# The second feed-forward product of a decoder layer by Strassen's scheme, with its sums on GpSimd

## The chip, the cores and the metric

The kernel runs on one core of one Trainium2 chip. The metric is the time of one execution on the device, in microseconds. The engines are TensorE (PE in the profile; its weight loads are PEld), VectorE (DVE), ScalarE (ACT), GpSimd (POOL), and SyncE (SP), which only issues loads and stores here.

## The reference, cut to what matters

One layer over 256 tokens of width 1024, float32: a mixer of attention and gated linear attention, cross-attention to 256 memory tokens, and a feed-forward block, with a layer norm behind each. The last part is what changes:

```python
D_MODEL, SEQ, D_FF = 1024, 256, 4096
DEEPNORM_ALPHA = 2.0 ** 0.25
def _sq_relu_mlp(h, w_ff1, w_ff2):
    return jnp.square(jax.nn.relu(h @ w_ff1)) @ w_ff2
ff = _sq_relu_mlp(x, w_ff1[l], w_ff2[l])
x = _layer_norm(DEEPNORM_ALPHA * x + ff, ln3_g[l], ln3_b[l])
```

## The kernel before, in words

**Precision.** Every large product is made of rounded operands (type fp32r) in three matmuls: ScalarE rounds a float32 tensor to its high part, VectorE subtracts that from the original to get the low part, and TensorE adds high x high, high x low and low x high (the helper `three`, L1374 to L1376). So each weight tile costs a load, one ScalarE pass and one VectorE pass before TensorE can use it. A "unit" is a load of 1 MB, 128 partitions x 2048; four buffers `raw` hold them, and a load waits until the low part of the unit four before it is made.

**The first product** (`ff1`, hidden = x @ w_ff1) goes by groups of 512 hidden columns. For each of four 128-wide blocks, 8 matmuls with 512 moving columns multiply the high weights by x's high and low parts at once, into the two halves of a bank (L1774), and 8 with 256 columns add the low weights (L1781). Banks 0 to 3 take the four blocks. ScalarE copies the small half out (L829), VectorE adds it to the other half from the bank (L1292), squares the positive part (L1295), and the two make high and low parts of the hidden blocks (L833, L1301).

**The second product** (`ff2`) adds each group's part to four banks, 4 to 7: two halves of the tokens (t) by two halves of the output columns (n), with four hidden tiles (k) and three matmuls each: 48 matmuls of 512 columns a group, 8 groups. The banks are started (seeded) with ALPHA x.

**Order.** Each engine runs its own list of instructions, with semaphores between them. The groups alternate: first product of group g+1, second product of group g; the weights of one are prepared while TensorE works on the other. The first group's first product is made in another form (`tokens`, hid0 and hid1) with a transpose. Six groups lie in a loop on each engine. GpSimd has no part in this stage but the inverse roots of the norms (L532). After the last matmul the layer norm of each half of the tokens ends the kernel (L1148 to L1165), and four stores.

## Time and profile before

| | |
|---|---|
| median of 3 runs | 406.27 us (405.71 to 406.28) |
| profiled execution, its span (its whole time is not on the page) | 404.4 us |
| TensorE busy | 397.4 us, 98% |
| VectorE busy | 286.5 us, 71% |
| ScalarE busy | 208.2 us, 51% |
| GpSimd busy | 64.7 us, 16% |
| loads and stores | 75.68 MB, mean 187 GB/s |

Busy time is the time in which an engine executes something; the span runs from the first instruction to the last. The chain that ended last is followed back from the last instruction, at each step to what released it. A matmul's duration (0.39 us) overlaps the next one's, so what counts for TensorE is the distance between starts.

### The profile page before, as it was taken

What the parts mean: (1) busy time and instruction counts of PE and PEld (TensorE: products, weight loads), DVE (VectorE), ACT (ScalarE), POOL (GpSimd) and SP (SyncE); (2) the same over time, 40 slices, a digit from 0 to 9 for tenths busy, and PEclk for the clock granted to TensorE, in tenths of its full rate; (3) what the DMA queues carried; (4) which work ended last, traced back from release to release, by engine and by line L of the source; (5) the groups of instructions that cost most, each with busy time, mean ns of one, the idle gap of its engine ahead of it and who ended that gap; (6) DMA issues with size and microseconds to landing.
All of it is one profiled execution on the core that took longest, in us unless ns stands there. A gap on an engine that the chain in (4) does not pass through costs nothing.

```text
span 404.4 us, 5680 instructions
## 1 busy us (share of the span) xinstructions
PE 397.4 (98%) x2148; PEld 341.3 (84%) x2148; DVE 286.5 (71%) x376; ACT 208.2 (51%) x295; POOL 64.7 (16%) x61
## 2 busy tenths in 40 slices
PE   9999999999999999999999999999999999999993
PEld 6888888888988888899888888888888888888882
DVE  5599584999987896878658858474656466574826
ACT  6666569566464627565743366353534434354500
POOL 2059300047951004000006000000000000000000
PEclk9999999999999999999999999999999999999999
DMA  8998727635635380827166173746465654644002
GB/s 287 376 352 281 254 106 264 255 105 174 243 109 205 108 309 0 311 105 245 68 209 201 46 273 117 256 155 212 199 207 207 207 207 150 237 141 198 0 0 104
DMA packets 31195, 75.68 MB, mean 187 GB/s; under 512 B 1510, under 2 KB 2886, under 8 KB 31174
## 3 DMA queue, kind: packets, MB, share of 16 engines
q1 hardware_dynamic: 30784, 75.24, 53.5%
q8 instruction: 13, 0.21, 0.2%
q10 hardware_dynamic: 390, 0.17, 0.2%
q14 instruction: 8, 0.07, 0.1%
HBM read 74.35 MB, written 1.05 MB: 186 GB/s over the span
## 4 chain that ended last, share of the span: by engine, by line
PE 98%; DVE 1%; DVEq 0%; issue 0%
PE bank L1374 18%; PE bank L1376 18%; PE bank L1375 18%; PE bank L1774 13%; PE bank L1448 12%; PE bank L1781 7%; PE bank L1452 6%; PE bank L1600 2%; PE bank L1380 1%; PE bank L1440 1%; PE bank L1554 1%; PE bank L1587 0%; PE bank L1653 0%; PE bank L1705 0%; PE bank L1546 0%; PE bank L1545 0%
## 5 line engine op out<-in xcount | busy, mean ns | idle before, releaser
L907 DVE TENSOR_TENSOR w_lo<-raw,w_hi 128x2048 fp32r<-128x2048 f32 x36 | 84.5, 2352 | 12.9 <-ACT w_hi L556 12.8
L556 ACT CAST w_hi<-raw 128x2048 fp32r<-128x2048 f32 x38 | 72.1, 1913 | 15.4 <-PE bank L1376 14.3
L1309 DVE TENSOR_TENSOR w_lo<-raw,w_hi 128x2048 fp32r<-128x2048 f32 x24 | 54.4, 2289 | 30.4 <-ACT w_hi L844 30.4
L1374 PE MATMUL bank<-w_hi,actB 128*128 128x512 f32 x192 | 75.6, 394 | 0.0
L1375 PE MATMUL bank<-w_lo,actB 128*128 128x512 f32 x192 | 74.9, 390 | 0.0
L1376 PE MATMUL bank<-w_hi,actB 128*128 128x512 f32 x192 | 74.8, 390 | 0.0
L844 ACT CAST w_hi<-raw 128x2048 fp32r<-128x2048 f32 x24 | 45.4, 1917 | 34.4 <-PE bank L1376 34.4
L1774 PE MATMUL bank<-actA,w_hi 128*128 128x512 f32 x224 | 52.2, 390 | 0.0
L1774 PEld LDWEIGHTS bank<-actA,w_hi 128*128 128x128 f32 x224 | 42.0, 188 | 8.7
L1376 PEld LDWEIGHTS bank<-w_hi,actB 128*128 128x128 f32 x192 | 36.1, 188 | 7.6
L1374 PEld LDWEIGHTS bank<-w_hi,actB 128*128 128x128 f32 x192 | 36.1, 188 | 7.2
L1375 PEld LDWEIGHTS bank<-w_lo,actB 128*128 128x128 f32 x192 | 36.1, 188 | 6.8
L1374 PE MATMUL bank<-w_hi,actA 128*128 128x512 f32 x96 | 38.0, 396 | 0.0
L1376 PE MATMUL bank<-w_hi,actA 128*128 128x512 f32 x96 | 37.5, 391 | 0.0
L1375 PE MATMUL bank<-w_lo,actA 128*128 128x512 f32 x96 | 37.5, 390 | 0.0
L532 POOL TENSOR_TENSOR rstd<-vareps,minus_half 128x1 f32<-128x1 f32 x6 | 3.3, 546 | 194.9 <-DVE vareps L1155 194.8
L1448 PE MATMUL bank<-actA,w_hi 128*128 128x512 f32 x140 | 34.3, 391 | 0.0
L1448 PEld LDWEIGHTS bank<-actA,w_hi 128*128 128x128 f32 x140 | 25.4, 188 | 4.6
L1781 PEld LDWEIGHTS bank<-actA,w_lo 128*128 128x128 f32 x224 | 27.8, 192 | 0.5
L1781 PE MATMUL bank<-actA,w_lo 128*128 128x256 f32 x224 | 28.0, 283 | 0.0
L829 ACT COPY att<-bank 128x256 f32<-128x256 f32 x28 | 9.6, 372 | 30.4 <-PE bank L1781 30.4
L1292 DVE TENSOR_TENSOR att<-bank,att 128x256 f32<-128x256 f32 x28 | 11.1, 421 | 16.3 <-ACT att L829 16.2
(198 smaller groups left out, 591.3 us busy)
## 6 DMA issues: line engine op xcount, KB each, us to landing
raw<-in_w_ff SPq DMA_DIRECT2D x32, 1024.0 KB, 5.4
raw<-in_w_in SPq DMA_DIRECT2D x10, 1024.0 KB, 6.4
raw<-in_w_xkv SPq DMA_DIRECT2D x8, 1024.0 KB, 5.0
raw<-in_w_mix_o SPq DMA_DIRECT2D x4, 1024.0 KB, 4.8
raw<-in_w_xq SPq DMA_DIRECT2D x4, 1024.0 KB, 4.9
raw<-in_w_xo SPq DMA_DIRECT2D x4, 1024.0 KB, 5.0
raw<-in_lead SPq DMA_DIRECT2D x6, 384.0 KB, 5.1
probs<-in_ln_g SPq DMA_DIRECT2D x3, 512.0 KB, 6.3
```

The lines of the kernel that those rows point to most:

```text
L556: act.copy(dst, half_view(u)).then_inc(hi_done, 1)
L844: act.copy(w_hi[:, (C_LOOP + k) % 2, half, :], raw[:, u % RAW, :]).then_inc(hi_done, 1)
L907: dve.tensor_tensor(dst, half_view(u), hi_part.bitcast(f32), ALU.subtract).then_inc(lo_done, 1)
L1292: dve.tensor_tensor(v, bank[2 * f + m][:, 0:S], v, ALU.add).then_inc(bank_free[2 * f + m], 1)
L1309: dve.tensor_tensor(w_lo[:, c % 2, half, :], raw[:, u % RAW, :], w_hi[:, c % 2, half, :].bitcast(f32), ALU.subtract).then_inc(lo_done, 1)
L1374: pe.matmul(dst, stat[0], mov[0], start=start, stop=False, skip_group_check=on)
L1375: pe.matmul(dst, stat[0], mov[1], start=False, stop=False, skip_group_check=on)
L1376: return pe.matmul(dst, stat[1], mov[0], start=False, stop=stop, skip_group_check=on)
L1448: pe.matmul(dst[:, :].rearrange("p (h s) -> p h s", h=2), weight(c, k, m * P, (m + 1) * P)[0], act[:, :, k, :], start=k == 0, stop=False, ...
L1452: return pe.matmul(dst[:, S:2 * S], weight(c, k, m * P, (m + 1) * P)[1], act[:, 0, k, :], start=False, stop=k == 7, skip_group_check=True)
L1774: pe.matmul(bank[m][:, :].rearrange("p (h s) -> p h s", h=2), w_hi[:, par, k // 4, a:a + P], actA[:, :, k, :], start=k == 0, stop=False, s ...
L1781: i = pe.matmul(bank[m][:, S:2 * S], w_lo[:, par, k // 4, a:a + P], actA_hi[:, k, :], start=False, stop=k == 7, skip_group_check=True)
```

## The change

Hidden tiles are taken in 16 pairs of k. For a pair, the left operand is a 2 x 2 arrangement of 128 x 128 blocks (two halves of the tokens, A1 and A2, by two k) and the right one is 2 x 2 blocks of 128 x 512. Instead of eight block products, seven are made (Strassen's scheme in Winograd's form), from raw blocks and from sums: S1 to S4 of hidden blocks, T1 to T4 of weight blocks. Each of the seven products adds up over the pairs in a bank of its own (0 to 6), and at the end VectorE combines the seven into the four corners of the output. The last pair is multiplied directly into the corners, with 24 matmuls. So pairs 0 to 14 have 21 matmuls for 24.

- GpSimd makes the sums T1 to T4 of each pair (four of 128 x 512) and S1 to S4 (four of 128 x 128), and adds the two halves of each first product's block (128 x 256, twice).
- ScalarE and VectorE make high and low parts of the sums too. The weights of the raw blocks B11, B22, B21 are rounded as one piece of 1536 columns; B12 itself is never multiplied but in the last pair. Rounding of the first product's weights goes in halves of 1024.
- The first product is made block by block, two blocks a pair (`up_block`), set between the products of the second. All blocks but one use bank 7, since seven banks hold products; ScalarE copies the whole bank into SBUF (`empty`) and so frees it.
- The weights are laid out on the host so that each load's partition row is contiguous. The loads are as many and as large as before.
- The loops are written out. The last norm takes the second half of the tokens first.

```diff
-G = 8
+PAIRS = 16
+A21, A11, A22, A12 = range(4)
+RAW_A, SUM_A = {"A11": 0, "A22": 1, "A12": 2}, {"S1": 3, "S2": 4, "S3": 5, "S4": 6}
+A_AT = {**RAW_A, **SUM_A}
+B_AT = {"B11": 0, "B22": 1, "B21": 2, "T1": 3, "T2": 4, "T4": 5, "T3": 6}
+PRODUCTS = {"P1": ("A11", "B11"), "P2": ("A12", "B21"), "P3": ("S4", "B22"), "P4": ("A22", "T4"),
+            "P5": ("S1", "T1"), "P6": ("S2", "T2"), "P7": ("S3", "T3")}
+P_BANK = {"P1": 0, "P2": 3, "P3": 2, "P4": 1, "P5": 4, "P6": 5, "P7": 6}
+FIRST_ORDER = ["P1", "P2", "P4", "P5", "P7", "P6", "P3"]
+ORDER = ["P1", "P2", "P3", "P4", "P5", "P6", "P7"]
+LAST_ORDER = ["P1", "P2", "P3", "P6", "P5", "P7", "P4"]
...
+FF_UNITS = [("down", 0), ("up", 2), ("up", 3), ("down", 1)]
+for _q in range(1, PAIRS - 2):
+    FF_UNITS += [("up", _q + 3), ("down", _q + 1)]
...
+        blocks = [flatB[:, 0:1792], flatB[:, 1792:3584], shared("probsT", 0, 1792)]
+        sums_w = probs[:, 0:2048]
+        down_hi = [again[:, at["values"]:at["values"] + 3584], w_hi[:, 0].rearrange("p h n -> p (h n)")[:, 0:3584]]
+        down_lo = [again[:, at["values"] + 3584:at["values"] + 7168],
+                   w_lo[:, 0].rearrange("p h n -> p (h n)")[:, 0:3584]]
...
+            def weight_sum(q, name):
+                u = ff_unit("down", q)
+                b12, b11, b22, b21 = [half_view(u)[:, n * 512:(n + 1) * 512] for n in range(4)]
+                t1, t2, t4, t3 = [sums_w[:, n * 512:(n + 1) * 512] for n in range(4)]
+                if name == "T1":
+                    pool.wait_ge(raw_in[u % RAW], raw_count(u))
+                    if q == 0:
+                        wait_full(pool, "cpv3")
+                    else:
+                        pool.wait_ge(wsum_lo, 2 * (q - 1) + 1)
+                    pool.tensor_tensor(t1, b12, b11, ALU.subtract).then_inc(wsum_made, 1)
+                elif name == "T2":
+                    pool.wait_ge(wsum_made, 4 * q + 1)
+                    pool.tensor_tensor(t2, b22, t1, ALU.subtract).then_inc(wsum_made, 1)
+                elif name == "T4":
+                    pool.wait_ge(wsum_made, 4 * q + 2)
+                    if q > 0:
+                        pool.wait_ge(wsum_lo, 2 * (q - 1) + 2)
+                    pool.tensor_tensor(t4, t2, b21, ALU.subtract).then_inc(wsum_made, 1)
+                else:
+                    pool.tensor_tensor(t3, b22, b12, ALU.subtract).then_inc(wsum_made, 1)
+            def add_halves(p, m):
+                n = 2 * (p - 2) + m
+                pool.wait_ge(up_free, n + 1)
+                pool.tensor_tensor(emptied[:, m, 0:S], emptied[:, m, 0:S], emptied[:, m, S:2 * S], ALU.add)\
+                    .then_inc(halves_added, 1)
+            def hidden_sums(p):
+                a21, a11, a22, a12, s1, s2, s3, s4 = [hidden[p % 2][:, n * P:(n + 1) * P] for n in range(8)]
+                if p < 2:
+                    wait_out(pool, "ht1")
+                else:
+                    pool.wait_ge(hidden_done, p - 1)
+                    pool.wait_ge(asum_lo, p - 1)
+                pool.tensor_tensor(s1, a21, a22, ALU.add).then_inc(asum_made, 1)
+                pool.wait_ge(asum_made, 4 * p + 1)
+                pool.tensor_tensor(s2, s1, a11, ALU.subtract).then_inc(asum_made, 1)
+                pool.tensor_tensor(s3, a11, a21, ALU.subtract).then_inc(asum_made, 1)
+                pool.wait_ge(asum_made, 4 * p + 2)
+                pool.tensor_tensor(s4, a12, s2, ALU.subtract).then_inc(asum_made, 1)
...
+            for q in range(1, PAIRS - 2):
+                hidden_sums(q + 1)
+                weight_sum(q + 1, "T1")
+                add_halves(q + 2, 0)
+                weight_sum(q + 1, "T2")
+                weight_sum(q + 1, "T4")
+                weight_sum(q + 1, "T3")
+                add_halves(q + 2, 1)
...
+            def empty(p, m):
+                n = 2 * (p - 2) + m
+                act.wait_ge(up_full, n + 1)
+                if n >= 2:
+                    act.wait_ge(hidden_done, p - 2)
+                act.copy(emptied[:, m], bank[6 if n == 1 else 7][:, :]).then_inc(up_free, 1)
...
+            for q in range(1, PAIRS - 2):
+                hidden_high(q + 1)
+                up_high(q + 3, 0)
+                empty(q + 2, 0)
+                asum_high(q + 1)
+                down_high(q + 1)
+                up_high(q + 3, 1)
+                empty(q + 2, 1)
+                wsum_high(q + 1, 0)
+                wsum_high(q + 1, 1)
...
-            def square(f, small, free):
-                for m in range(2):
-                    v = relu[:, f, m * S:(m + 1) * S]
-                    dve.wait_ge(small_done, small + (2 * f + m + 1))
-                    dve.tensor_tensor(v, bank[2 * f + m][:, 0:S], v, ALU.add).then_inc(bank_free[2 * f + m], 1)
-                for m in range(2):
-                    dve.wait_ge(bank_free[2 * f + m], free[2 * f + m])
-                dve.scalar_tensor_tensor(relu[:, f, :], relu[:, f, :], 0.0, relu[:, f, :], ALU.max, ALU.mult)\
-                    .then_inc(sq_done, 1)
...
+            def wsum_low(q, half):
+                cut = slice(1536 + 1024 * half, 2560 + 1024 * half)
+                dve.wait_ge(wsum_hi, 2 * q + half + 1)
+                dve.tensor_tensor(down_lo[q % 2][:, cut], sums_w[:, 1024 * half:1024 * (half + 1)],
+                                  down_hi[q % 2][:, cut].bitcast(f32), ALU.subtract).then_inc(wsum_lo, 1)
+            def square(p):
+                dve.wait_ge(halves_added, 2 * (p - 2) + 2)
+                dve.wait_ge(a_lo, p - 1)
+                dve.wait_ge(asum_lo, p - 1)
+                v = emptied[:, :, 0:S]
+                dve.scalar_tensor_tensor(hidden[p % 2][:, 0:512].rearrange("p (m s) -> p m s", m=2), v, 0.0, v,
+                                         ALU.max, ALU.mult).then_inc(hidden_done, 1)
...
+            for q in range(1, PAIRS - 2):
+                wsum_low(q, 0)
+                wsum_low(q, 1)
+                hidden_low(q + 1)
+                up_low(q + 3, 0)
+                asum_low(q + 1)
+                down_low(q + 1)
+                up_low(q + 3, 1)
+                square(q + 2)
+            wsum_low(PAIRS - 2, 0)
...
+            b = product("P2")
+            dve.wait_ge(p1_copied, 1)
+            dve.tensor_tensor(b, b, first_product, ALU.add).then_inc(corner_done, 1)
+            link(dve.tensor_tensor(first_and_sixth, product("P6"), first_product, ALU.add))
+            link(dve.tensor_tensor(with_fifth, product("P5"), first_and_sixth, ALU.add))
+            b = product("P3")
+            dve.tensor_tensor(b, b, with_fifth, ALU.add).then_inc(corner_done, 1)
+            link(dve.tensor_tensor(with_seventh, product("P7"), first_and_sixth, ALU.add))
+            link(dve.scalar_tensor_tensor(left_rest, X[:, 0, 0:512], ALPHA, with_seventh, ALU.mult, ALU.add))
+            dve.tensor_tensor(bank[P_BANK["P7"]][:, :], product("P5"), left_rest, ALU.add).then_inc(corner_done, 1)
+            b = product("P4")
+            dve.tensor_tensor(b, with_seventh, b, ALU.subtract).then_inc(corner_done, 1)
...
+            def up_block(p, m, between=None):
+                n = 2 * (p - 2) + m
+                b = bank[6 if n == 1 else 7]
+                if n == 0:
+                    wait_out(pe, "yt11")
+                elif n == 1:
+                    wait_out(pe, "yt10")
+                else:
+                    pe.wait_ge(up_free, 1 if n == 2 else n)
+                hi, lo = (v[:, 1, p % 2, :].rearrange("p (k n) -> p k n", k=8) for v in (w_hi, w_lo))
+                for k in range(8):
+                    if m == 0 and k % 4 == 0:
+                        pe.wait_ge(up_hi, 2 * (p - 2) + k // 4 + 1)
+                    pe.matmul(b[:, :].rearrange("p (h s) -> p h s", h=2), hi[:, k, m * P:(m + 1) * P], actA[:, :, k, :],
+                              start=k == 0, stop=False, skip_group_check=True)
+                if between is not None:
+                    between()
+                for k in range(8):
+                    if m == 0 and k % 4 == 0:
+                        pe.wait_ge(up_lo, 2 * (p - 2) + k // 4 + 1)
+                    i = pe.matmul(b[:, S:2 * S], lo[:, k, m * P:(m + 1) * P], actA_hi[:, k, :],
+                                  start=False, stop=k == 7, skip_group_check=True)
+                i.then_inc(up_full, 1)
+            def multiply(q, names, last=False):
+                for name in names:
+                    a, b = PRODUCTS[name]
+                    pe.wait_ge(a_lo, q + 1)
+                    if a in SUM_A:
+                        pe.wait_ge(asum_lo, q + 1)
+                    if B_AT[b] < 3:
+                        pe.wait_ge(down_raw_lo, q + 1)
+                    else:
+                        pe.wait_ge(wsum_lo, 2 * q + (B_AT[b] - 3) // 2 + 1)
+                    to = bank[P_BANK[name]]
...
+                    fresh = q == 0 and name in ("P1", "P5", "P6", "P7")
+                    cut_a, cut_b = slice(A_AT[a] * P, (A_AT[a] + 1) * P), slice(B_AT[b] * 512, (B_AT[b] + 1) * 512)
+                    i = three(to[:, :], [blocks[q % 3][:, cut_a], blocks[q % 3][:, 896:1792][:, cut_a]],
+                              [v[q % 2][:, cut_b] for v in (down_hi, down_lo)], fresh, False, on=True)
+                    if last:
+                        i.then_inc(product_done, 1)
+                if not last and name == "P7" or name == "P3" and q == 0:
+                    i.then_inc(pair_used, 1)
+            up_block(2, 0, between=lambda: transpose_hidden(0))
+            transpose_hidden(1)
+            up_block(2, 1)
+            multiply(0, FIRST_ORDER)
+            for q in range(1, PAIRS - 2):
+                up_block(q + 2, 0)
+                multiply(q, ORDER[:3])
+                up_block(q + 2, 1)
+                multiply(q, ORDER[3:])
+            multiply(PAIRS - 2, LAST_ORDER, last=True)
+            pe.wait_ge(a_lo, PAIRS)
+            pe.wait_ge(up_lo, 2 * (PAIRS - 2) + 2)
+            final = blocks[(PAIRS - 1) % 3]
+            for n, (name, t, c) in enumerate([("P2", 1, 1), ("P3", 1, 0), ("P7", 0, 0), ("P4", 0, 1)]):
+                pe.wait_ge(corner_done, n + 1)
+                for m in range(2):
+                    block_at = (2 * m + t) * P
+                    i = three(bank[P_BANK[name]][:, :], [final[:, at0 + block_at:at0 + block_at + P] for at0 in (0, 896)],
+                              [v[:, 1, 0, m * 1024 + c * 512:m * 1024 + (c + 1) * 512] for v in (w_hi, w_lo)],
+                              False, m == 1, on=True)
+                i.then_inc(corner_full, 1)
```

How the order of instructions moves. TensorE, inside the stage: before, one group's first product runs over four banks without a break, and its second product follows.

```order
L1774 MATMUL bank<-actA,w_hi 128x512 [waits bank_free1]
L1774 MATMUL bank<-actA,w_hi 128x512 x7
L1774 MATMUL bank<-actA,w_hi 128x512 [waits bank_free2]
L1774 MATMUL bank<-actA,w_hi 128x512 x7
L1774 MATMUL bank<-actA,w_hi 128x512 [waits bank_free3]
L1774 MATMUL bank<-actA,w_hi 128x512 x7
L1781 MATMUL bank<-actA,w_lo 128x256 x32
```

TensorE, now, from the second up block of one pair on (`up_free` is raised by ScalarE's copy out of bank 7; `wsum_lo`, `asum_lo` and `a_lo` by VectorE's low parts of T, of S and of the raw hidden blocks):

```order
L1963 MATMUL bank<-actA,w_hi 128x512 [waits up_free]
L1963 MATMUL bank<-actA,w_hi 128x512 x7
L1970 MATMUL bank<-actA,w_lo 128x256 x8
L1558 MATMUL bank<-w_hi,actB 128x512 [waits wsum_lo,a_lo]
L1559 MATMUL bank<-w_lo,actB 128x512
L1560 MATMUL bank<-w_hi,actB 128x512
L1558 MATMUL bank<-w_hi,actB 128x512 [waits wsum_lo,asum_lo,a_lo]
L1559 MATMUL bank<-w_lo,actB 128x512
L1560 MATMUL bank<-w_hi,actB 128x512
```

Each block of the first product now waits for the copy of the block before it, and each product names the low parts that it needs.

VectorE, one half of a group before, inside its loop:

```order
L1292 TENSOR_TENSOR att<-bank,att 128x256 [waits small_done]
L1294 REGISTER_ALU
L1295 SCALAR_TENSOR_TENSOR att<-att 128x512 [waits bank_free3,bank_free2]
L1308 REGISTER_ALU
L1309 TENSOR_TENSOR w_lo<-raw,w_hi 128x2048 [waits hi_done]
L1299 REGISTER_ALU
L1301 TENSOR_TENSOR actB<-att,actB 128x512 [waits hid_hi]
```

VectorE, one pair now (`const` here is the tensor that the bank was copied into, `probs` the T sums, `qk` the hidden blocks and S sums):

```order
L1437 TENSOR_TENSOR w_lo<-probs,w_hi 128x1024 [waits wsum_hi] x2
L1452 TENSOR_TENSOR actB<-qk,actB 128x384 [waits a_hi]
L1424 TENSOR_TENSOR w_lo<-raw,w_hi 128x1024 [waits up_hi]
L1457 TENSOR_TENSOR actB<-qk,actB 128x512 [waits asum_hi]
L1430 TENSOR_TENSOR again<-raw,again 128x1536 [waits down_raw_hi]
L1424 TENSOR_TENSOR w_lo<-raw,w_hi 128x1024 [waits up_hi]
L1445 SCALAR_TENSOR_TENSOR qk<-const 128x512 [waits asum_lo,a_lo,halves_added]
```

The additions that read a bank are gone from VectorE's list, and every instruction left in it reads tensors in SBUF only.

GpSimd, which before had only three inverse roots after the last of its rounding work, now has ten instructions for each pair:

```order
L604 TENSOR_TENSOR qk<-qk 128x128 [waits asum_lo,hidden_done]
L606 TENSOR_TENSOR qk<-qk 128x128 [waits asum_made]
L607 TENSOR_TENSOR qk<-qk 128x128
L609 TENSOR_TENSOR qk<-qk 128x128 [waits asum_made]
L578 TENSOR_TENSOR probs<-raw 128x512 [waits wsum_lo,raw_in1]
L593 TENSOR_TENSOR const<-const 128x256 [waits up_free]
L581 TENSOR_TENSOR probs<-raw,probs 128x512 [waits wsum_made]
L586 TENSOR_TENSOR probs<-probs,raw 128x512 [waits wsum_lo,wsum_made]
L588 TENSOR_TENSOR probs<-raw 128x512
L593 TENSOR_TENSOR const<-const 128x256 [waits up_free]
```

They stand between the square of one pair, which the first of them waits for, and the square of the next, which waits for the last.

## Rows read from the trace of the kernel before

**Rows 1.** The page: busy time by engine, and the chain that ended last.

```profile
PE 397.4 (98%) x2148; PEld 341.3 (84%) x2148; DVE 286.5 (71%) x376; ACT 208.2 (51%) x295; POOL 64.7 (16%) x61
...
PE 98%; DVE 1%; DVEq 0%; issue 0%
```

**Rows 2.** Chain in order of time: start us, duration us, engine, tile, line, count.

```profile
232.43 5.45 PE bank L1774 x24
...
299.31 7.25 PE bank L1774 x32
...
321.30 7.25 PE bank L1774 x32
...
372.54 3.83 PE bank L1781 x32
```

**Rows 3.** Groups by line from 230 to 400: busy us, mean ns, idle before.

```profile
L1309 DVE TENSOR_TENSOR w_lo<-raw,w_hi 128x2048 fp32r<-128x2048 f32 x24 | 54.4, 2289 | 30.4 <-ACT w_hi L844 30.4
...
L844 ACT CAST w_hi<-raw 128x2048 fp32r<-128x2048 f32 x24 | 45.4, 1917 | 34.4 <-PE bank L1376 34.4
...
L1301 DVE TENSOR_TENSOR actB<-att,actB 128x512 fp32r<-128x512 f32 x14 | 9.7, 689 | 4.8 <-ACT actB L833 4.8
...
L833 ACT CAST actB<-att 128x512 fp32r<-128x512 f32 x14 | 8.7, 624 | 8.9 <-DVE att L1295 8.9
...
L671 ACT ACTIVATE bank<-X 128x512 f32<-128x512 f32 x4 | 2.2, 602 | 0.0
```

**Rows 4.** Groups by line, whole span, GpSimd's longer forms.

```profile
L516 POOL TENSOR_TENSOR w_lo<-raw,w_hi 128x1024 fp32r<-128x1024 f32 x4 | 9.8, 2472 | 56.1 <-ACT w_hi L556 54.0 <-DVE X L1165 2.1
...
L497 POOL TENSOR_TENSOR qk<-gla,qk 128x256 f32<-128x256 f32 x1 | 0.8, 753 | 0.0
```

**Rows 5.** Timeline around 100, 105 and 115: start us, duration us, instruction.

```profile
100.13 2.28 DVE L907 TENSOR_TENSOR w_lo<-raw,w_hi 128x2048 fp32r<-128x2048 f32 x1
...
100.75 2.24 POOL L495 TENSOR_TENSOR qk<-gla,qk 128x256 f32<-128x256 f32 x1 [0.59 <-PE bank L1600]
...
104.69 2.29 DVE L907 TENSOR_TENSOR w_lo<-raw,w_hi 128x2048 fp32r<-128x2048 f32 x1
104.90 2.78 POOL L495 TENSOR_TENSOR qk<-gla,qk 128x256 f32<-128x256 f32 x1
...
115.15 2.55 POOL L511 TENSOR_TENSOR gla<-gla,gnorm 128x512 f32<-128x512 f32 x2
...
116.55 3.29 DVE L907 TENSOR_TENSOR w_lo<-raw,w_hi 128x2048 fp32r<-128x2048 f32 x1 [1.49 <-ACT w_hi L556]
```

**Rows 6.** The same view around 25 and from 210.

```profile
24.68 5.26 POOL L469 TENSOR_SCALAR probsT<-const 128x384 f32<-128x384 f32 x3 [21.92 <-DMA const<-in_consts]
25.03 2.31 DVE L907 TENSOR_TENSOR w_lo<-raw,w_hi 128x2048 fp32r<-128x2048 f32 x1
...
210.80 2.29 DVE L907 TENSOR_TENSOR w_lo<-raw,w_hi 128x2048 fp32r<-128x2048 f32 x1 [4.96 <-ACT w_hi L556]
...
212.66 2.69 POOL L516 TENSOR_TENSOR w_lo<-raw,w_hi 128x1024 fp32r<-128x1024 f32 x1 [53.99 <-ACT w_hi L556]
...
215.96 2.41 POOL L516 TENSOR_TENSOR w_lo<-raw,w_hi 128x1024 fp32r<-128x1024 f32 x1
...
216.61 1.40 DVE L1165 SCALAR_TENSOR_TENSOR X<-bank,rstd,probsT 128x512 f32<-128x512 f32 x2
```

**Rows 7.** The end: timeline, then a stretch (us, busy by engine, granted clock).

```profile
397.77 0.39 PE L1376 MATMUL bank<-w_hi,actB 128*128 128x512 f32 x1
398.20 0.70 DVE L1148 BATCH_NORM_STATS2 stats<-bank 128x6 f32<-128x512 f32 x1 [1.07 <-PE bank L1376]
...
400.56 1.40 DVE L1165 SCALAR_TENSOR_TENSOR X<-bank,rstd,probsT 128x512 f32<-128x512 f32 x2
...
402.50:403.00 0.50, 0.00 (x0) 0.00 (x0) 0.00 (x0) 0.00 (x0) 0.00 (x0) 0.63 1.03 377
```

**Rows 8.** The page's loads: KB each, us to landing.

```profile
raw<-in_w_ff SPq DMA_DIRECT2D x32, 1024.0 KB, 5.4
```

More of the change, by code:

```diff
@@ L144 @@
              10: "mo11", 11: "xv11", 12: "xq11", 13: "xq3", 15: "xo11", C_FF1_0: "hid1"}
-ROWS_END = {9: 1, 14: 2, C_FF2_0: 3}
-FF_BASE = [sum(b == bank for b, _ in FILL.values()) for bank in range(8)]
+ROWS_END = {9: 1, 14: 2}
 def build(nc, x, lead, memT, w_in, w_glr, w_gate_up, b_gate, gla_norm_g, w_mix_o, ln1_g, ln1_b, w_xq, w_xkv,
@@ new lines, in _ @@
+            inverse_root(0, 0, 0)
+            inverse_root(0, 1, 1)
+            pool.wait_ge(ln_done, 4)
+            for half in range(2):
+                lo_half(unit(12, 1), half)
+            lo_half(unit(C_FF1_0, 1), 0)
+            inverse_root(1, 0, 0)
+            lo_half(unit(C_FF1_0, 1), 1)
+            wait_out(pool, "yt01")
+            pool.wait_ge(xT_hi, 6)
+            sl = (slice(None), slice(4, 8), slice(0, P))
+            pool.tensor_tensor(actA_lo[sl], yT_half, actA_hi[sl].bitcast(f32), ALU.subtract)\
+                .then_inc(yT_lo, 1)
@@ new lines, in hidden_high, with asum_high @@
+            def hidden_high(p):
+                if p < 2:
+                    wait_out(act, "ht1")
+                else:
+                    act.wait_ge(hidden_done, p - 1)
+                if p >= 3:
+                    act.wait_ge(pair_used, p - 2)
+                width = 384 if p < PAIRS - 1 else 512
+                act.copy(blocks[p % 3][:, 0:width], hidden[p % 2][:, 512 - width:512]).then_inc(a_hi, 1)
+            def asum_high(p):
+                act.wait_ge(asum_made, 4 * p + 4)
+                act.copy(blocks[p % 3][:, 384:896], hidden[p % 2][:, 512:1024]).then_inc(asum_hi, 1)
@@ L876, in _ @@
[L876 to L892 removed]
+            act.wait_ge(ln_done, 8)
@@ L895, in _ @@
+            act.copy(first_product, bank[P_BANK["P1"]][:, :]).then_inc(p1_copied, 1)
         @block.vector
@@ L1355, in _ @@
-            for t in range(2):
-                layer_norm(2, t, [(bank[4 + 2 * t + c], (bank_full[4 + 2 * t + c], FF_BASE[4 + 2 * t + c] + 1), bank_free[4 + 2 * t + c])
-                                  for c in range(2)])
+            up_low(3, 0)
+            hidden_low(0)
+            hidden_low(1)
+            asum_low(0)
+            down_low(1)
+            asum_low(1)
+            up_low(3, 1)
+            square(2)
+            for q in range(1, PAIRS - 2):
[7 more added lines that the diff above has]
+                square(q + 2)
@@ L1805, in need @@
-            def need(c):
-                return [lo_count(unit(c, half)) for half in range(2)]
-            ff1(C_FF1_1 % 2, need(C_FF1_1), FF_BASE, between=transpose_hidden)
-            ff2(0, C_FF2_0 % 2, need(C_FF2_0), first=True)
-            with pe.Fori(0, G // 2 - 1) as i:
-                for g in range(2):
-                    c = C_LOOP + 2 * g
-                    ff1(c % 2, [i * 8 + n for n in need(c)], [i * 2 + (n + 1 + g) for n in FF_BASE])
-                    ff2(1 - g, (c + 1) % 2, [i * 8 + n for n in need(c + 1)], i * 4 + (2 + 2 * g))
```

389 lines of the change are left out of this document (192 added, 197 removed).

## The prediction, on record before the kernel was run

> **What bounds the kernel now.** I read the page's busy shares first, then its chain of waits, then the chain in order of time, and only then the helpers. TensorE is busy for 397.4 of 404.4 us and the chain that ended last lies on it for 98% [rows 1]. In the feed-forward stage the chain repeats every 22.0 us (321.30 − 299.31) with nothing but matmuls in it [rows 2]; a 512-column matmul follows the next after 7.25/32 = 0.2266 us, a 256-column one after 3.83/32 = 0.120 us. A stage group holds two pairs of hidden tiles, so a pair costs 11.0 us of TensorE. VectorE and ScalarE wait there for TensorE, not the other way: 30.4 us of idle time before the low parts, 34.4 us before the high parts [rows 3]. GpSimd is busy for 64.7 us of the whole span. So matmuls taken out shorten the end as long as the helpers keep up, and the whole question is whether they do.
>
> **What the change takes off TensorE.** Each pair had 8 block products of 3 matmuls; 15 of the 16 pairs now have 7. That is 45 matmuls fewer: 45 × 0.2266 = 10.2 us. A pair is then 16 × 0.2266 + 16 × 0.120 + 21 × 0.2266 = 10.3 us. This is the whole gain on offer, 404.4 − 10.2 = 394.2.
>
> **What each pair costs the helpers.** Durations of forms that the trace lacks I take between its rows. VectorE: 2048 wide is 2.29, 512 wide 0.69 [rows 3], so 1.22 for 1024, 1.76 for 1536, 0.56 for 384. A pair has four of 1024 (two weight halves, two halves of the T sums), one of 1536, one of 384, the S sums and the square at 512: 4.88 + 1.76 + 0.56 + 1.38 = 8.6 us. ScalarE: 2048 is 1.92, 512 is 0.62, the copy of a bank 0.60 [rows 3]; four of 1.05, 1.49, 0.52, 0.62 and two bank copies: 8.0 us. GpSimd: four T sums of 512, two additions of the halves at 256, four S sums of 128. 512 wide is 2.55/2 = 1.27 [rows 5], 256 wide is 0.75, 1024 wide 2.4 to 2.7 [rows 4]; 128 wide isn't in the trace: it is at least half of the 0.59 that 256 columns hold the memory (below), and at most the 0.75 of a whole 256 wide one. I take 0.31 held and 0.45 in all, on the line through 256 and 512: 5.1 + 1.5 + 1.8 = 8.4 us. Each is under 10.3 us, so three separate engines would just keep up.
>
> **They are not separate.** All of GpSimd's new instructions read two tensors in SBUF, and so do all eight of VectorE's per pair; the two banks' additions that VectorE read from PSUM are gone to ScalarE and GpSimd. The trace shows what such pairs do to each other [rows 5]. VectorE's low part runs from 100.13 to 102.41; GpSimd's product starts at 100.75, takes 2.24 instead of 0.75 and ends at 102.99, 0.58 after VectorE. Again at 104.90: 2.78, ending 0.70 after VectorE's end at 106.98. The other way round, GpSimd is busy until 117.70, and the low part that VectorE issued at 116.55 takes 3.29 instead of 2.29 and ends 2.14 later. At 212.66 GpSimd's 1024 wide piece ends at 215.35, 2.26 after VectorE's [rows 6]. So they take turns by whole instructions; only about 0.1 of start-up overlaps. Where VectorE reads one bank of PSUM there is no loss: 1.40 for two at 216.61 beside GpSimd's 2.41 at 215.96 [rows 6]. Against it stands one place: VectorE's 2.31 at 25.03 wasn't held up by GpSimd's one-input scaling from 24.68 [rows 6]; but that form is not in the new loop.
>
> The Trainium skill (SBUF — State Buffer, "Who interferes with whom") says that a VectorE instruction with two SBUF inputs and a GpSimd instruction that reads SBUF share an interface, and that the first one keeps it for the whole instruction. By that rule taken literally a pair is 8.6 + 8.4 = 17.0 us; by the rows, where start-up overlaps, it is less, and the sum goes by the rows.
>
> Held times from those rows: VectorE 2.14 per 2048 columns, so 7040 columns a pair are 7.35 us. GpSimd 2.26 per 1024, 0.59 per 256, so 1.15, 0.59 and 0.31: 4.6 + 1.18 + 1.24 = 7.0 us. Together 14.4 us a pair, if no moment is lost, against 10.3 of TensorE.
>
> **The period worked out.** Zero is the end of a square. VectorE's next low part (first half of T) goes at once, to 1.1; then they alternate: S1 to 1.4, second half of T 2.5, S2 2.8, low of the raw blocks 3.2, S3 3.5, a weight half 4.6, S4 4.9. ScalarE rounds the S sums 5.0 to 5.6. GpSimd's T1 to 6.2, low of the S sums 6.7, first addition of halves 7.3, the 1536 wide low part 8.9, T2 10.1, the other weight half 11.1, T4 12.3, T3 13.55, second addition 14.3, square 14.4 to 15.05. So I take 15.05 us a pair; the ends are 14.4 and 17.0. TensorE waits 4.75 of it, in two places: about 1 before the first up block and 3.7 before the second, since every up block but one writes bank 7 and ScalarE's copy out of it stands behind the rounding that follows the square.
>
> **The sum.** Before the loop little changes: TensorE starts the next up group at 232.3 [rows 2], does two blocks (5.5), the transposes (0.8) and pair 0 (21 × 0.2266 = 4.8) to 243.4, with 0.5 of waiting for the S sums. The helpers are behind by then. The last transposed block is out of its bank at about 236.6; GpSimd, taking turns, has eight S sums (5.2, to 241.8), two additions of halves (1.3), T4 and T3 beside a VectorE piece (3.2, to 246.3), and the square of pair 2 ends at 247.0. Twelve more periods of 15.05 give 427.6. From there the last square 15.05, two T low parts and the last raw one (3.0, GpSimd now idle), eight combinations of 0.65 (5.25) of which the corners' matmuls hide none at the end of VectorE's queue, two norms of 4.5 and 4.4 (stats 1.3, two small ones 0.35, 1.4, 1.4, as in the old tail [rows 7]), and from VectorE's end to the end of the span 404.4 − 401.96 = 2.4 [rows 7]: 34.6, span 462.2. In place of the old tail of 6.4 us behind the last matmul it is about 9, because VectorE combines products when TensorE could already be done. Other way: 394.2 + 13 × 4.75 = 456, + 2.7 tail, + 3 waited in the last pair = 462. The page gives the profiled execution no time but its span of 404.4, 1.9 under the median 406.27; with that added the forecast is 464. Loads: 1 MB lands in 5.4 us [rows 8] and a pair needs two, each asked for a full period ahead: nothing. A weight row is now contiguous, which can only help what is hidden.
>
> **Rivals.** (1) Taking turns does not hold for these instructions: then helpers at 8.0 to 8.6 of 10.3 keep up, TensorE sets the end, 394.2 + 2.7 of tail + 1 + 1.9 = 400, faster. For: the place at 25.03; against: four places of just these forms. (2) They take turns only in part, or the small sums cost less than pro rata: 12.7 a pair, 464 − 13 × 2.35 = 433. (3) No start-up overlaps, or 128-wide sums cost their upper bound: 17.0 a pair, 464 + 25 = 489. (4) The clock. TensorE's last matmul ends at 398.16; the mean granted clock from 402.50 to 403.00 is 0.63 [rows 7], so it fell from its full 2.4 GHz to the lower level of 1.2 at about 402.6, 4.5 us later. A wait of 3.7 us per pair is near to that. If it fell in each, an up block of 2.8 us would be 5.5; TensorE has 4.75 us of slack in a pair, so one block costs little, but at half clock throughout a pair is 20.6 us: somewhere between 464 and 530, I put 495. The Trainium skill (TensorE: Matmul & The Clock Gate, "The HAM clock gate") has idle time as the cause of just this fall; the row agrees, and no row of before shows a wait inside the loop long enough to try it.
>
> **How the numbers follow.** Forecast 464 with 0.76, for which 455 (no moment lost) to 480 is the likely range; (1) 0.04, (2) 0.06, (3) 0.07, (4) 0.07. Range 446 to 488: it leaves out (1), (2) and about half of (3) and (4), near 2 in 10. A difference of 0.2% (0.8 us) is about what a measurement tells from none. Faster only by (1): 0.04; within 0.2%: 0.01, for something between (1) and (2); slower 0.95.
>
> **What would show it.** Right: in the loop GpSimd's 512 wide sums last well over 1.27 on average, VectorE's 1024 wide ones over 1.22, and their ends never fall inside one another; both are busy or waiting nearly all of the period; a period near 15 us; TensorE's share falls to some 84% of the span (387 of 462 us), with its waits on the bank that ScalarE empties. Wrong: a period of 10.3 with the durations of the rows (rival 1); a granted clock under 1 in the loop (rival 4); or TensorE waiting mostly for a load.

## The result, and the profile after

The changed kernel takes 466.5 us (466.2 to 466.8, 4 runs), the kernel before 406.13 us beside it: a ratio of 1.149, 95% interval 1.148 to 1.151. The forecast was 464. The profiled execution has a span of 464.4 us, against 462.2 worked out.

The page of the changed kernel, busy time by engine and then the shares of the chain that ended last, answers to [rows 1]:

```profile
PE 411.7 (89%) x2103; PEld 344.6 (74%) x2103; DVE 355.1 (76%) x416; ACT 247.8 (53%) x357; POOL 269.1 (58%) x209
...
PE 50%; POOL 35%; DVE 6%; issue 6%; DMA 1%; ACT 1%; DVEq 0%; POOLq 0%
```

The 45 matmuls are gone (2148 to 2103), and so is the chain that lay on TensorE for 98%: 35% of the time to the end is now GpSimd's. Its groups and VectorE's in the loop, by line, from 245 to 445 us (busy us, mean ns, idle before):

```profile
L1424 DVE TENSOR_TENSOR w_lo<-raw,w_hi 128x1024 fp32r<-128x1024 f32 x27 | 51.7, 1915 | 0.0
L581 POOL TENSOR_TENSOR probs<-raw,probs 128x512 f32<-128x512 f32 x13 | 36.6, 2819 | 0.0
L586 POOL TENSOR_TENSOR probs<-probs,raw 128x512 f32<-128x512 f32 x14 | 29.8, 2128 | 1.0
...
L593 POOL TENSOR_TENSOR const<-const 128x256 f32<-128x256 f32 x26 | 25.0, 961 | 0.0
...
L609 POOL TENSOR_TENSOR qk<-qk 128x128 f32<-128x128 f32 x13 | 18.7, 1437 | 0.0
...
L1437 DVE TENSOR_TENSOR w_lo<-probs,w_hi 128x1024 fp32r<-128x1024 f32 x14 | 18.3, 1348 | 0.0
L578 POOL TENSOR_TENSOR probs<-raw 128x512 f32<-128x512 f32 x13 | 17.0, 1309 | 0.0
```

Equal forms have unequal durations: GpSimd's sums of 512 columns take 1.31 (T1), 2.13 (T4) or 2.82 us (T2), a sum of 128 columns (S4) takes longer than the T1 of 512, and VectorE's subtraction of 1024 columns takes 1.35 or 1.92. The work sets the shortest of each; what is above it is waiting inside the instruction, as the experiments below show. The timeline of one period shows whom each waits for (start us, duration us, instruction, idle before it):

```profile
338.74 0.69 DVE L1445 SCALAR_TENSOR_TENSOR qk<-const 128x512 f32<-128x512 f32 x1 [3.15 <-POOL const L593]
339.35 2.61 DVE L1437 TENSOR_TENSOR w_lo<-probs,w_hi 128x1024 fp32r<-128x1024 f32 x2
...
339.51 1.37 POOL L604 TENSOR_TENSOR qk<-qk 128x128 f32<-128x128 f32 x1 [0.80 <-DVE qk L1445]
...
341.46 2.11 PE L1963 MATMUL bank<-actA,w_hi 128*128 128x512 f32 x8 [2.84 <-ACT const L949]
...
346.49 1.97 DVE L1430 TENSOR_TENSOR again<-raw,again 128x1536 fp32r<-128x1536 f32 x1 [0.24 <-ACT again L931]
346.81 2.82 POOL L581 TENSOR_TENSOR probs<-raw,probs 128x512 f32<-128x512 f32 x1
...
347.93 2.14 PE L1963 MATMUL bank<-actA,w_hi 128*128 128x512 f32 x8 [0.67 <-ACT const L949]
348.38 2.32 DVE L1424 TENSOR_TENSOR w_lo<-raw,w_hi 128x1024 fp32r<-128x1024 f32 x1
...
349.70 2.15 POOL L586 TENSOR_TENSOR probs<-probs,raw 128x512 f32<-128x512 f32 x1
```

T2 (L581) is issued at 346.81, inside VectorE's 1536-wide instruction, which ends at 348.46; T2 ends at 349.63, 1.17 after it. The weight half that VectorE issued at 348.38 then takes 2.32 and ends at 350.70, 1.07 after T2; T4 ends at 351.85, 1.15 after that. In the trace the recorded spans overlap, but the ends stand one behind the other, each by about the time that its own work takes: what overlaps is the waiting. It is the pattern of [rows 5], now all through the loop. The square of the next pair starts at 353.84, so the period is 15.10 us.

What the engines wait for, from 245 to 445 us (total us, times, longest):

```profile
DVE qk L1445 <- POOL const L593: 40.8, 13, 3.2
PE bank L1963 <- ACT const L949: 36.7, 16, 3.0
```

And busy time by engine over three periods (stretch, its us, busy, granted clock in the third number from the right):

```profile
338.74:353.84 15.10, 11.21 (x53) 8.74 (x53) 10.71 (x8) 7.46 (x10) 14.14 (x10) 1.00 0.35 136
353.84:368.93 15.09, 12.26 (x53) 9.95 (x53) 10.69 (x8) 7.47 (x10) 14.13 (x10) 0.89 0.37 143
368.93:384.04 15.11, 11.22 (x53) 8.75 (x53) 10.73 (x8) 7.46 (x10) 14.15 (x10) 1.00 0.37 136
```

GpSimd is busy 14.1 of 15.1 us. The 13 periods of the loop last 15.08 to 15.12 us, the last one 15.00, whatever the clock of TensorE.

### The profile page after: what moved, and what is told of

Its sections match the earlier page's. It is cut to its first block, busy times and chain, and to the rows that moved or that the text cites. A ratio compares the mean times of both kernels' runs of the same rounds, so it can differ in the third digit from the quotient of the medians.

```text
span 464.4 us, 5838 instructions
## 1 busy us (share of the span) xinstructions
PE 411.7 (89%) x2103; PEld 344.6 (74%) x2103; DVE 355.1 (76%) x416; ACT 247.8 (53%) x357; POOL 269.1 (58%) x209
## 4 chain that ended last, share of the span: by engine, by line
PE 50%; POOL 35%; DVE 6%; issue 6%; DMA 1%; ACT 1%; DVEq 0%; POOLq 0%
PE bank L1632 10%; PE bank L1558 9%; PE bank L1560 9%; PE bank L1559 9%; POOL probs L581 8%; POOL probs L586 6%; PE bank L1636 5%; POOL qk L609 4%; POOL qk L604 4%; POOL qk L606 4%; POOL probs L578 4%; POOL probs L588 4%; DVE qk L1445 2%; POOL const L593 2%; PE bank L1784 1%
## 5 line engine op out<-in xcount | busy, mean ns | idle before, releaser
L1963 PE MATMUL bank<-actA,w_hi 128*128 128x512 f32 x224 | 69.2, 459 | 36.7 <-ACT const L949 36.7
L1963 PEld LDWEIGHTS bank<-actA,w_hi 128*128 128x128 f32 x224 | 47.7, 220 | 53.8 <-ACT const L949 43.6
L1040 DVE TENSOR_TENSOR w_lo<-raw,w_hi 128x2048 fp32r<-128x2048 f32 x30 | 70.6, 2359 | 5.8 <-ACT w_hi L643 5.6
L643 ACT CAST w_hi<-raw 128x2048 fp32r<-128x2048 f32 x32 | 60.7, 1913 | 11.5 <-PE bank L1560 9.3
L1424 DVE TENSOR_TENSOR w_lo<-raw,w_hi 128x1024 fp32r<-128x1024 f32 x30 | 57.4, 1916 | 0.0
L1558 PE MATMUL bank<-w_hi,actB 128*128 128x512 f32 x107 | 42.5, 397 | 0.0
L1559 PE MATMUL bank<-w_lo,actB 128*128 128x512 f32 x107 | 41.8, 391 | 0.0
L1560 PE MATMUL bank<-w_hi,actB 128*128 128x512 f32 x107 | 41.7, 390 | 0.0
L581 POOL TENSOR_TENSOR probs<-raw,probs 128x512 f32<-128x512 f32 x15 | 39.6, 2639 | 0.2
L1632 PE MATMUL bank<-actA,w_hi 128*128 128x512 f32 x140 | 34.4, 391 | 0.0
L586 POOL TENSOR_TENSOR probs<-probs,raw 128x512 f32<-128x512 f32 x15 | 31.1, 2074 | 1.1
L919 ACT CAST w_hi<-raw 128x1024 fp32r<-128x1024 f32 x30 | 31.2, 1044 | 0.0
```

The source lines that it names most:

```text
L581: pool.tensor_tensor(t2, b22, t1, ALU.subtract).then_inc(wsum_made, 1)
L586: pool.tensor_tensor(t4, t2, b21, ALU.subtract).then_inc(wsum_made, 1)
L643: act.copy(dst, half_view(u)).then_inc(hi_done, 1)
L1040: dve.tensor_tensor(dst, half_view(u), hi_part.bitcast(f32), ALU.subtract).then_inc(lo_done, 1)
L1424: dve.tensor_tensor(w_lo[:, 1, p % 2, cut], half_view(ff_unit("up", p))[:, cut], w_hi[:, 1, p % 2, cut].bitcast(f32), ALU.subtract).then_i ...
L1558: pe.matmul(dst, stat[0], mov[0], start=start, stop=False, skip_group_check=on)
```

## The experiments

The theory: VectorE's and GpSimd's instructions that read two tensors in SBUF (the memory on the chip that the engines work from; the banks lie in another one, PSUM) take turns by whole instructions, and the period is made up of the times for which each holds the other off, with little else. The rivals: GpSimd's own chain is too long whatever VectorE does; VectorE has too much work; TensorE's order with one bank for the up blocks costs the time; or the reading is not what matters, only that GpSimd is at work. The kernel before took 405.7 to 405.8 us beside these runs. Periods are from one square to the next.

**One side made short.** In the first, GpSimd's ten instructions of a pair stay, but cover 16 columns; the rest is left out.

```diff
+                if q > 0:
+                    b12, b11, b22, b21, t1, t2, t4, t3 = [v[:, 0:16] for v in (b12, b11, b22, b21, t1, t2, t4, t3)]
...
-                pool.tensor_tensor(emptied[:, m, 0:S], emptied[:, m, 0:S], emptied[:, m, S:2 * S], ALU.add)\
+                pool.tensor_tensor(emptied[:, m, 0:16], emptied[:, m, 0:16], emptied[:, m, S:S + 16], ALU.add)\
```

> From the second use of each buffer on, GpSimd's sums and additions are cut to 16 columns (the rest of them isn't computed); the order, the waits and VectorE's work stay. Theory A (GpSimd's and VectorE's two-input instructions exclude each other): VectorE's 1024 wide low parts fall from a mean of 1.9 to 1.22 us, the 1536 wide from 1.97 to 1.76, the period of a pair from 15.1 to TensorE's 10.3, the time to 466.5 - 13 x 4.8 = 404 or a little less (400 to 405), the wait for bank 7 nearly gone. Rival B (the single bank 7 and the chain of hand-overs between engines set the period, whatever the durations): above 12.5 us a pair, 433 or more.

In the second, VectorE's subtractions and the square are cut so, and GpSimd's work is whole.

```diff
-                cut = slice(half * 1024, (half + 1) * 1024)
+                cut = slice(half * 1024, half * 1024 + 16)
...
-                width = 384 if p < PAIRS - 1 else 512
+                width = 16
```

> VectorE's low parts and its square are cut to 16 columns in the stage of pairs (the rest isn't computed), GpSimd keeps its whole work. Theory A: GpSimd's 512 wide sums take 1.30 each (now 1.31, 2.82, 2.13, 1.39), the 128 wide 0.45 (now 0.77 to 1.44), the 256 wide 0.75 (now 0.97); 8.4 us in all, plus hand-overs: 10.3 a pair, 400 to 405 us. Rival C (GpSimd is that slow by itself in this stage, from its operands or from the loads that write the same buffers): its durations stay, period about 14, time about 452.

And in the third both.

> Both cuts at once (neither GpSimd's sums nor VectorE's low parts are computed beyond 16 columns): what TensorE alone makes of the new order. Period 10.3. The prediction's parts: 394.2 + 2.7 for the longer tail + 1 + 1.9 outside of the span = 400. If TensorE's saving of 45 matmuls did not come, or the order cost more by itself (the wait for bank 7), over 406.

Measured: 399.35 us (ratio 0.984, 0.982 to 0.986), 399.38 (0.984, 0.982 to 0.986) and 399.2 (0.984, 0.982 to 0.986). The first two lie 0.6 us under their range of 400 to 405. Cutting either side alone gives all of it back, and cutting both gives nothing more. Neither engine is the bound with its own work: it is the two together. At a period of 10.4 us TensorE is the bound again, and these 399 us are what the fewer matmuls are worth, near the 400 of rival 1. Groups by line of the first (GpSimd short), from 245 to 370 us:

```profile
L1428 DVE TENSOR_TENSOR w_lo<-raw,w_hi 128x1024 fp32r<-128x1024 f32 x25 | 30.8, 1231 | 0.0
...
L613 POOL TENSOR_TENSOR qk<-qk 128x16 f32<-128x16 f32 x12 | 14.3, 1194 | 0.0
```

of the second (VectorE short):

```profile
L1424 DVE TENSOR_TENSOR w_lo<-raw,w_hi 128x16 fp32r<-128x16 f32 x25 | 20.1, 805 | 18.3 <-ACT w_hi L919 18.3
...
L593 POOL TENSOR_TENSOR const<-const 128x256 f32<-128x256 f32 x24 | 17.8, 740 | 17.8 <-ACT const L949 17.8
L578 POOL TENSOR_TENSOR probs<-raw 128x512 f32<-128x512 f32 x13 | 17.0, 1309 | 0.0
...
L609 POOL TENSOR_TENSOR qk<-qk 128x128 f32<-128x128 f32 x13 | 6.0, 462 | 0.0
```

and of the third:

```profile
L611 POOL TENSOR_TENSOR qk<-qk 128x16 f32<-128x16 f32 x12 | 2.7, 223 | 0.0
...
L1428 DVE TENSOR_TENSOR w_lo<-raw,w_hi 128x16 fp32r<-128x16 f32 x25 | 4.4, 176 | 19.3 <-ACT w_hi L923 19.3
```

Undisturbed, VectorE's 1024 columns are 1.23 us and GpSimd's 128, 256 and 512 columns are 0.46, 0.74 and 1.30 (worked out before: 1.22; 0.45, 0.75, 1.27). The clearest rows are those of 16 columns: a sum of GpSimd takes 0.22 us when VectorE's instructions are short too and S4 takes 1.19 beside VectorE's full ones; VectorE's subtraction takes 0.18 and, beside GpSimd's full sums, 0.81. So each waits for the other. These durations also rule out that the period is only a chain of semaphores from engine to engine: such waits stand in the profile as idle time ahead of an instruction, and here the instructions themselves are longer.

**Reading, or only being at work?** From the second pair on, GpSimd's sums are replaced by fills of a scratch tile, which read nothing, in the same chain of semaphores; the sums are left out.

```diff
+                    i = pool.memset(scratch[:, :], 0.0)
...
-                    pool.tensor_tensor(t2, b22, t1, ALU.subtract).then_inc(wsum_made, 1)
+                    pool.tensor_tensor(t2, b22, t1, ALU.subtract).then_inc(wsum_made, 1) if q == 0 else fill(4, wsum_made, 4 * q + 2)
```

> GpSimd's sums are replaced by fills of a scratch tensor that take about as long (4 fills of 352 columns for a 512 wide sum, 2 for an addition of halves, 1 for a 128 wide sum; the sums are not computed), with the same waits: GpSimd is as busy and reads nothing. Theory A with the page's condition that GpSimd must read: VectorE's 1024 wide low parts 1.22, period 10.3 to 11.2 (GpSimd's own list), time 402 to 414. If any busy GpSimd hinders VectorE, whether it reads or not: low parts stay near 1.9, about 15 a pair, 460 and more.

Measured: 423.7 us (1.044, 1.042 to 1.046), period 12.0. That is above the 402 to 414 expected, so the expectation missed. A second version has 14 fills a pair in place of 24.

> As e4_gpsimd_writes_only, in which GpSimd fills a scratch tile in place of its sums in SBUF from the second pair on (so the sums are left out), but with 14 fills of a pair in place of 24. There 24 linked fills took the whole period of 12.00 us, 0.50 us each. If GpSimd's own chain was what held that kernel at 423.7 us, 14 fills take 7.0 us of a pair and the period falls to TensorE's 10.4 us, as in the two kernels with short sums: 399 to 401 us. If a GpSimd that only writes does hinder VectorE, the period stays between 10.8 and 12, 405 to 420 us, and VectorE's 1024-wide instruction shows more than 1.22 us in its mean.

Measured: 399.95 us (0.985, 0.984 to 0.987), period 10.4. Groups by line of the kernel with 24 fills, from 245 to 370 us:

```profile
L575 POOL MEMSET scratch<- 128x352 f32 x252 | 98.9, 393 | 26.8 <-DVE qk L1460 7.8
...
L1439 DVE TENSOR_TENSOR w_lo<-raw,w_hi 128x1024 fp32r<-128x1024 f32 x21 | 25.6, 1217 | 0.0
```

and of the one with 14, from 310 to 400:

```profile
L575 POOL MEMSET scratch<- 128x352 f32 x92 | 36.1, 393 | 33.3 <-ACT const L964 22.2 <-DVE qk L1460 4.7
...
L1439 DVE TENSOR_TENSOR w_lo<-raw,w_hi 128x1024 fp32r<-128x1024 f32 x13 | 15.8, 1219 | 0.0
```

The miss was my filler, not the theory: 24 linked fills of 0.50 us each were a chain of 12 us. In both, VectorE's 1024 columns take 1.22 us, and no fill takes less than 0.387 or more than 0.403 us: a GpSimd that only writes does not hold VectorE up, and is not held up.

**One input in place of two.** GpSimd scales one tensor, 430, 240 and 128 columns wide, in place of its sums.

```diff
-                    pool.tensor_tensor(t4, t2, b21, ALU.subtract)
+                    pool.tensor_scalar(t4[:, 0:430], t2[:, 0:430], 1.0, None, ALU.mult)
```

> GpSimd's sums are replaced by scalings with one input, shorter so that each should last as long alone (430 columns for a 512 wide sum, 240 and 128 for the others; the sums are not computed). If a GpSimd instruction that reads one tensor holds VectorE off for its whole length, the period stays about 15 and VectorE's 1024 wide low parts near 1.9. If it holds only for a short part, as the one place at 25 us in the trace of before looks, VectorE's durations are near 1.3, GpSimd still waits for VectorE, and the period is 11 to 13, the time 410 to 440.

Measured: 435.4 us (1.073, 1.071 to 1.075), period 12.85. Groups by line, 245 to 370 us:

```profile
L1424 DVE TENSOR_TENSOR w_lo<-raw,w_hi 128x1024 fp32r<-128x1024 f32 x20 | 28.6, 1431 | 0.0
L586 POOL TENSOR_SCALAR probs<-probs 128x430 f32<-128x430 f32 x10 | 18.7, 1870 | 0.7
...
L604 POOL TENSOR_SCALAR qk<-qk 128x128 f32<-128x128 f32 x10 | 14.3, 1434 | 7.3 <-DVE qk L1445 7.3
```

It lies between: 1.43 us in place of 1.92 for VectorE's weight half, 1.87 in place of 2.13 for what stands in T4's place. GpSimd itself still waits: the 128 columns of L604 take 1.43, with two inputs 1.37. So a GpSimd instruction with one input holds VectorE off too, for a part of the time. That fits neither the place in [rows 6] where VectorE's 2.31 us lost nothing nor the full turn-taking. What sets the part is not shown.

**Fewer turns.** TensorE adds the two halves of an up block in the same half of the bank, so GpSimd has eight instructions a pair in place of ten and ScalarE copies half a bank; the sums are unchanged.

```diff
-                    pe.matmul(b[:, :].rearrange("p (h s) -> p h s", h=2), hi[:, k, m * P:(m + 1) * P], actA[:, :, k, :],
+                    for act in (actA_hi, actA_lo):
+                        pe.matmul(b[:, 0:S], hi[:, k, m * P:(m + 1) * P], act[:, k, :],
```

> The changed kernel with one part of GpSimd's work gone by another way: the first product's small terms are added by TensorE into the same half of the bank (three matmuls of 256 columns for one of 512 and one of 256), so the two additions of halves go and ScalarE copies 256 columns. The result is whole. TensorE 10.5 a pair. Theory A: two turns fewer, 2 x 0.59 held and about 0.1 each of hand-over: 15.1 - 1.4 = 13.7 a pair, 448 us. Rival B (bank 7): ScalarE's copy comes back by 0.2 earlier only, 14.9 a pair, 463.

Measured: 444.7 us (1.096, 1.094 to 1.098), period 13.56. The two turns are worth 1.54 us a pair. 2 × 0.59 held is 1.18 of it; the other 0.36 isn't traced to its place. Rival B's 14.9 a pair is ruled out.

**The sums on VectorE.** GpSimd has nothing in the loop.

```diff
-                    pool.tensor_tensor(t2, b22, t1, ALU.subtract).then_inc(wsum_made, 1)
+                    dve.tensor_tensor(t2, b22, t1, ALU.subtract).then_inc(wsum_made, 1)
```

> All sums and additions of halves move from GpSimd to VectorE, which then has 18 instructions a pair and GpSimd none. The result is whole. Theory A: since the two were never beside each other, and VectorE needs 1.04 ns a column where GpSimd holds the memory for 2.2, one engine alone is faster: 4 x 1.13 + 1.66 + 0.46 + 1.2 + 2.4 + 0.8 + 0.68 and 0.5 of own waits = 12.2 to 12.4 a pair, 466.5 - 13 x 2.7 = 431 us (426 to 438), faster than with both engines and slower than before. If the two engines had worked side by side, taking the work of one to the other could not shorten the period: 15.1 or more.

Measured: 426.6 us (1.052, 1.050 to 1.053), period 12.14. One engine that does all the work is 40 us faster than two that share it. With that and the edit before it:

> As v1_sums_on_vector, and the additions of halves left to TensorE as in e6_no_halves. The result is whole. VectorE's list: 11.7 a pair, 466.5 - 13 x 3.4 = 422 us; TensorE's 10.5 isn't reached, so still slower than before.

Measured: 415.7 us (1.025, 1.023 to 1.026), period 11.35. And with ScalarE taking the relu out of the bank and squaring:

```diff
-                act.copy(emptied[:, m, 0:S], bank[6 if n == 1 else 7][:, 0:S]).then_inc(up_free, 1)
+                act.activation(emptied[:, m, 0:S], bank[6 if n == 1 else 7][:, 0:S], ACT.Relu).then_inc(up_free, 1)
...
+                    act.activation(hidden[p % 2][:, 0:512].rearrange("p (m s) -> p m s", m=2), emptied[:, :, 0:S],
+                                   ACT.Square).then_inc(hidden_done, 1)
```

> The whole result is computed: as in v3_no_halves (all sums on VectorE, TensorE adds the small terms in the same half of the bank), and now ScalarE also takes the relu while it empties the bank and squares the hidden block; VectorE has no square. In v3_no_halves VectorE was busy 11.28 of a period of 11.35 us, and the square took 0.60 us of it (square at 246.35, next instruction at 246.95). If VectorE is the bound there, the period falls to 11.35 - 0.60 = 10.75 us and the time to 415.7 - 12 x 0.6 = 408.5 us (406 to 411), which is near the kernel before (405.8) but not clearly under it. If instead TensorE's feed or ScalarE's queue sets the period (ScalarE gets one instruction of about 0.6 us more on 7.05 us busy), it stays above 11.2 and the time above 413 us.

Measured: 409.1 us (1.008, 1.006 to 1.009), period 10.75. Two periods of it, in the columns of the stretches above:

```profile
330.55:341.29 10.74, 10.74 (x70) 9.74 (x69) 10.67 (x16) 7.60 (x10) 0.00 (x0) 1.00 0.52 197
341.29:352.05 10.76, 10.76 (x70) 9.74 (x69) 10.69 (x16) 7.61 (x11) 0.00 (x0) 1.00 0.50 194
```

VectorE is busy 10.67 of 10.74 us, and TensorE has no idle time left either. This loop is shorter than the 11.0 us a pair of [rows 2], yet the kernel is 3 us slower than before. The end takes part of it: the span ends 8.5 us after the last matmul (399.21 to 407.7), since VectorE combines the seven products there, and 6.2 us in the kernel before (398.16 to 404.4, [rows 7]). Where the loop begins, TensorE is idle 2.2 us between 232 and 252, and in the last pair it waits 1.5 and 0.4 us more for VectorE; it did neither before. That is 6.4 us lost against about 13 × 0.25 = 3.2 won in the loop. No version with a whole result is faster than the kernel before. What is left to take from VectorE in the last one's loop is some 0.2 us a pair: by the distances of [rows 2], TensorE needs 48 × 0.120 + 21 × 0.2266 = 10.5 with the halves added by its matmuls.

## Why the prediction was right, step by step

**TensorE's saving.** Right. With the helpers out of the way the kernels take 399.2 to 399.4 us and the period is 10.4, against 400 and 10.3.

**Three engines that would just keep up.** Right, now as measured durations: 4 × 1.30 + 2 × 0.74 + 4 × 0.46 = 8.5 us of GpSimd a pair (8.4 worked out), and a period of TensorE's length (10.4) when VectorE's work is short, and the same the other way.

**Turn-taking.** Right, and it is the cause: shown by cutting either side, by the sum of 16 columns that takes 1.19 us, by the fills that read nothing, and by the 40 us won when one engine does the work of both. GpSimd's ten instructions last 14.1 us a pair in place of 8.5. The Trainium skill (SBUF — State Buffer, "Who interferes with whom") has the first one keep the interface for its whole instruction. The order of ends agrees; the literal sum of 17.0 us does not, since 15.10 was measured. What it leaves out is the start-up beside the other's hold; the prediction's held times, without it, gave 14.4.

**The period.** 15.10 against 15.05. The order of turns was worked out right in the places that carry the time: T2 and T4 behind VectorE's 1536- and 1024-wide pieces, the second addition ahead of the square. The waits of TensorE came out at 0.67 and 2.84 us before the two up blocks, where the prediction had about 1 and 3.7. Its idle time in a full-clock period is 15.10 − 11.21 = 3.9 in place of 4.75. Part of the difference is that the busy time counts each matmul to its own end, 0.39 us, where the next follows after 0.23: ahead of a wait that adds 0.16 to it.

**The start.** The one term that was clearly mis-sized: the square of pair 2 ends at 248.80 in place of 247.0. The sum had it behind GpSimd's T3, and there it stands, but T3 ends at 248.26 in place of 246.3. GpSimd's and VectorE's lines of the timeline:

```profile
241.36 2.95 POOL L593 TENSOR_TENSOR const<-const 128x256 f32<-128x256 f32 x2
241.70 2.01 DVE L1430 TENSOR_TENSOR w_lo<-raw,w_hi 128x1536 fp32r<-128x1536 f32 x1 [1.05 <-ACT w_hi L931]
243.63 1.22 DVE L1457 TENSOR_TENSOR actB<-qk,actB 128x512 fp32r<-128x512 f32 x1
244.27 1.75 POOL L586 TENSOR_TENSOR probs<-probs,raw 128x512 f32<-128x512 f32 x1
244.78 2.31 DVE L1424 TENSOR_TENSOR w_lo<-raw,w_hi 128x1024 fp32r<-128x1024 f32 x1
245.97 2.29 POOL L588 TENSOR_TENSOR probs<-raw 128x512 f32<-128x512 f32 x1
247.01 1.79 DVE L1445 SCALAR_TENSOR_TENSOR qk<-const 128x512 f32<-128x512 f32 x1
```

The sum had the two additions of halves without VectorE beside them, 1.3 us. VectorE's 1536-wide low part took its turn between them, so they took 2.95 and ended at 244.31, 1.2 late. T4 and T3 had one VectorE piece beside them in the sum (3.2 us), and in the trace the low parts of the S sums and a weight half (3.95). The theory was the same; what failed here is the order of turns, which had been worked out in full only for the loop. The square was issued at 247.01, inside T3, and so lasts 1.79 in place of 0.69. These 1.8 us, and 196.24 in place of 13 × 15.05 = 195.65 for the loop, are the 2.2 of difference in the span, less 0.2 at the end.

**The end.** From the end of the last square, at 445.04, to the end of the span is 19.4 us; worked out: 34.6 − 15.05 = 19.55. Behind the last matmul it is 8.3 us (456.13 to 464.4), where the prediction had about 9.

**TensorE's share.** 84% was expected and the page has 89%. This part was wrong. TensorE is busy 411.7 us in place of 387, for two causes of about equal size. At full clock it is busy 11.2 us of a period, not 10.3 (see the period above), and a fall of the clock adds about 1 us to a period that has one, 12.26 for 11.21.

**The clock, rival 4.** It did fall, in 10 of the 13 periods, and cost next to nothing. The prediction had named a granted clock under 1 in the loop as a sign of being wrong; it came, and did not mean that. An example: after a wait of 2.99 us, TensorE starts an up block at 356.56; its eight pieces take 3.40 us in place of 2.11. A line of the timeline and one of another period, then stretches of 1 us (granted clock third from the right):

```profile
356.56 3.40 PE L1963 MATMUL bank<-actA,w_hi 128*128 128x512 f32 x8 [2.99 <-ACT const L949]
...
432.06 3.68 PE L1963 MATMUL bank<-actA,w_hi 128*128 128x512 f32 x8 [2.83 <-ACT const L949]
```

```profile
356.00:357.00 1.00, 0.44 (x2) 0.39 (x3) 1.00 (x2) 0.51 (x2) 0.94 (x1) 1.00 1.04 442
357.00:358.00 1.00, 1.00 (x4) 0.76 (x3) 1.00 (x3) 0.00 (x0) 1.00 (x2) 0.53 0.34 139
...
360.00:361.00 1.00, 1.00 (x8) 1.00 (x8) 0.81 (x1) 1.00 (x2) 1.00 (x2) 0.76 0.00 0
```

The clock is at 2.4 GHz until 357, when TensorE was already at work again, then at 1.2, and back from some 360.5 on. Of the other falls, one came after a wait of only 1.77 us (281.03), one after 2.83 (432.06), while the waits of 2.84 at 341.46 and 371.65 had none. So the prediction's comparison with a fall after 4.5 us erred: much shorter waits do it, and the length of the wait alone does not tell which. A period with a fall lasts 15.09 us and the one before, without, 15.10: TensorE's slack of 3.9 us covers the loss. Only at the end can it have cost something: a fall from 445.8 to 449.2, in and behind a wait of 4.80 us, lies on the way to VectorE's combinations, and VectorE waits there 0.21 us for a product. The Trainium skill (TensorE: Matmul & The Clock Gate, "The HAM clock gate") ties the fall to idle time; the rows agree in that each fall stands beside a wait, and 2.83 with a fall and 2.84 without show that there is more to it. In the page of the profile the lower clock shows as busy time, which is one reason why 89% of busy TensorE does not mean a bound here.

**What the experiments missed by.** Three forecasts were 3 to 7 us too high: 448 (measured 444.7), 431 (426.6, inside its range) and 422 (415.7). They took the gain of a period 13 times from 466.5. The start gained too: the square of pair 2 ends at 247.3, 247.7 and 247.0 in these three, where the changed kernel has 248.80. The rest is the period itself, 13.56 for 13.7, 12.14 for 12.4 and 11.35 for 11.7; no working was given for the 11.7. The version with ScalarE's square, forecast from a measured 415.7 and a measured 0.60 us, came out within 0.6 us of 408.5.
